# Prompt attention heads issued two at a time, and two key buffers exchanged, in a two-layer decoder step

## The chip, the core and the metric

The kernel runs on one core of a Trainium2 chip. The metric is the device time of one execution in microseconds (us), as a median over runs. The engines named are TensorE (PE for its matmuls, PEld for its weight loads), VectorE (DVE), ScalarE (ACT), GpSimd (POOL) and SyncE (SP, which here only issues transfers).

## What is computed

One inference step of a two-layer decoder for a prompt of 256 tokens and eight sequences of eight new tokens each, 320 tokens in all, with d_model 2048. A layer is an input projection, three mixers side by side, an output projection, and a feed-forward part:

```python
h   = rms_norm(x, norm1[l])
q, k, v, z, xbc, dt_raw, xp = jnp.split(h @ w_in[l], SPLITS, axis=-1)
o_sb   = stick_breaking_attention(q, k_all, v_all, pos0, sb_bias[l])   # 8 heads of 64
y_ssd  = ...   # Mamba2 chunked scan, 16 heads
y_pool = ...   # pooling over windows of 2, 4, 8, 16
x = x + jnp.concatenate([o_sb, y_ssd, y_pool], axis=-1) @ w_out[l]
x = x + (silu(conv3(rms_norm(x) @ w_gate)) * (rms_norm(x) @ w_up)) @ w_down
```

The attention has no softmax. For a query block, z = q k / 8 + bias, masked; the weight of a key is exp(log_sigmoid(z) + later), where `later` sums the masked log_sigmoid(-z) of the keys behind it; the output is weights times values. The prompt attends to itself; each of the eight sequences attends to 2048 cached keys and values as well, which lie in pages of 128 rows that a page table names.

## The kernel before

**Products.** Activations lie transposed, tiles of 128 features by 320 tokens. A weight block of 1024 by 256 numbers (1 MB) is a *unit*: SyncE loads it into one of four raw slots, ScalarE makes its rounded high part (`wh`), VectorE the rest (`wl`), and TensorE makes three products per 128x128 tile (L1183 to L1185: high by high, high by low, low by high), 48 instructions a unit. Four units are a *body*. `wh` and `wl` hold two units, so ScalarE and VectorE work a bounded way ahead of TensorE.

**Input stage of a layer.** Nine bodies follow one another: three of q, k, v, three of the scan's input, two of its gate, one of the pool's input (`B_XP`). Between the units, numbered u = 0 to 35 on every engine, the prompt's attention is done by a function `heads(u)` that each engine has for itself. For head n: TensorE makes the scores at u = 10 + 2n (`head_z`: a 256-column and a 128-column matmul over 64 partitions, into bank 4 or 5), VectorE copies them out with the bias at u = 12 + 2n (`head_in`, L1975, into one of four buffers `hbuf`), ScalarE takes the logarithms at 13 + 2n, VectorE the softplus at 14 + 2n, TensorE its running sums at 14 + 2n (`head_sums`, L1321 to L1324), VectorE the argument at 16 + 2n, ScalarE the exponential at 17 + 2n, TensorE the outputs at 18 + 2n (`head_out`, L1347 to L1349: three 128-column matmuls into one half of bank 7's partitions), and VectorE takes them at 20 + 2n (`head_take`). Every step waits by semaphore for the one before; the program order is fixed on each engine.

**Mixing stage.** Then the cached keys are gone through in 16 chunks of eight pages. A chunk's keys lie in one of two rings of eight pages: even chunks in `kring0`, over the later part of the residual x, odd ones in `kring1`, over raw slots 0 and 1. GpSimd stores the covered part of x to memory before (`x_stored`), SyncE brings it back after (`x_back`, L537). A page of keys is loaded into a ring slot once the page two chunks before has been transposed (`k_T`, counted over all pages; transposes at L1427). Values come page by page into one ring of eight, `vring`, from GpSimd's queue, each slot refilled once TensorE has used it (L1471). The scan's and the pool's steps are laid between by a table (`MIX`); among them L1529 and L1594.

**The way out.** The first body of w_out is loaded by SyncE in four transfers, `first_out(0)` to `first_out(3)`. The first two go to raw slots 0 and 1 and wait until chunk 15's first four, then all its pages have been transposed. The third waits for the last scores and arguments, then x comes back, then the engines meet and the fourth is issued. VectorE waits for `x_back` after that meeting, ahead of its split of the fourth (`out_lo(3)`, L2273).

Of the kernel before, what the change touches and what calls it, by code (L numbers as in the profile page):

```python
# [27 lines left out]
P = 128  # L28
# [102 lines left out]
def build(nc, a, o):  # L131

    with ExitStack() as ctx:
# [74 lines left out]
        kring = [sb_at("kring0", [P, RING, SBW], F32, x_at + 4096), sb_at("kring1", [P, RING, SBW], F32, raw_at)]  # L208
        x_late = x[:].rearrange("p k t -> p (k t)")[:, 1024:1024 + RING * SBW]
        x_kept = nc.dram_tensor("x_kept", (P, RING * SBW), F32, kind="Internal").ap()  # L210
# [219 lines left out]

        def tokens(blk):

            return (blk * P, P) if blk < 2 else (SEQ, SAMP)
# [6 lines left out]
        def _(sync):  # L440
# [21 lines left out]
            for l in range(DEPTH):  # L462
# [26 lines left out]
                for k in range(RING):  # L489
                    key_in(0, k)  # L490
# [13 lines left out]
                for q in range(1, CHUNKS):  # L504
                    for k in range(RING):
                        slot = RING * (q - 2) + k
                        if q == 1:
# [20 lines left out]
                sync.wait_ge(k_T, l * (CHUNKS * 8) + CHUNKS * 8 - 4)  # L528
                first_out(0)
                sync.wait_ge(k_T, l * (CHUNKS * 8) + CHUNKS * 8)  # L530
# [3 lines left out]
                first_out(2)  # L534
                for k in range(RING):
                    sync.wait_ge(v_loaded[k], (l + 1) * (16 * CHUNKS))
                sync.dma_start(x_late, x_kept).then_inc(x_back, 16)  # L537
# [29 lines left out]
        def _(pool):  # L567
# [37 lines left out]
            for l in range(DEPTH):  # L605
# [4 lines left out]
                pool.dma_start(x_kept, x_late).then_inc(x_stored, 16)  # L610
# [180 lines left out]
        def _(act):  # L791
# [104 lines left out]
            for l in range(DEPTH):  # L896
# [13 lines left out]
                def head_logs(n):  # L910
                    act.wait_ge(z_out, l * 8 + n + 1)
                    act.activation(za[:, n % 2, :], hbuf[:, n % 4, :], ACT.Abs)
# [3 lines left out]
                def head_weights(n):  # L916
                    act.wait_ge(z_arg, l * 8 + n + 1)
                    act.activation(hbuf[:, n % 4, :], hbuf[:, n % 4, :], ACT.Exp).then_inc(z_w, 1)
# [241 lines left out]
        def _(pe):  # L1160
# [87 lines left out]
            for l in range(DEPTH):  # L1248
# [55 lines left out]
                def head_z(n):  # L1304

                    pe.wait_ge(qk_ready, l + 1)
                    if n >= 2:
                        pe.wait_ge(z_out, l * 8 + (n - 1))
                    r, b = slice(DH * (n % 2), DH * (n % 2) + DH), ps[4 + n % 2]
                    pe.matmul(b[:, 0:SEQ], k[r, n // 2, 0:P], q[r, n // 2, 0:SEQ], start=True, stop=True)  # L1310
                    pe.matmul(b[:, SEQ:SEQ + P], k[r, n // 2, P:SEQ], q[r, n // 2, P:SEQ], start=True, stop=True
                              ).then_inc(z_mm, 1)
# [26 lines left out]
                def head_out(n):  # L1339
                    pe.wait_ge(z_w, l * 8 + (n + 1))  # L1340
                    if n:
                        pe.wait_ge(o_out, l * 8 + n)
# [1148 lines left out]
```

## Time and profile before

| | us |
|---|---|
| median of 3 runs | 3234.13 |
| lowest, highest | 3229.59, 3236.45 |
| profiled execution | 3232.32 |
| its span | 3230.7 |
| TensorE busy in the span | 3144.0 |
| VectorE, ScalarE busy | 1897.0, 1347.1 |

The profile gives, for one execution, each engine's busy time, the chain of waits that ended last (followed back from the last instruction to what released it), who waited for whom, and the instructions in order of time. In a timeline a line is start, duration, engine, line of the kernel, operation, output and inputs, shapes and count; in square brackets is the time that the engine stood idle before it and who ended that. Matmuls are pipelined: their durations overlap, and the distance of two starts is what one takes of the queue. One full matmul of 32-bit numbers leaves two records, a transpose one.

### The profile page before, as it was taken

To read this page: it belongs to the slowest core of one execution; us is meant where nothing else is said; L and a number is where in the kernel's file an instruction comes from. 1 tells how busy PE (TensorE), PEld (TensorE's weight loads), DVE (VectorE), ACT (ScalarE), POOL (GpSimd) and SP (SyncE) were. 2 spreads that over 40 slices of the span, in tenths; PEclk is the share of its full clock that TensorE was granted. 3 is DMA by queue.
4 is the path that set the end of the run, shared out by engine and by line. 5 is a ranking of instruction groups with operands and counts; after the bars stand their busy time and mean duration, and the time that the engine had idled before them with its cause. 6 is when DMAs were issued, how large, how long until landed. Compare 5 with 4: busy or idle time off the path is not lost.

```text
span 3230.7 us, 62291 instructions
## 1 busy us (share of the span) xinstructions
PE 3144.0 (97%) x23688; PEld 3005.7 (93%) x23688; DVE 1897.0 (59%) x3335; ACT 1347.1 (42%) x1663; POOL 432.7 (13%) x543
## 2 busy tenths in 40 slices
PE   8999998999999999999999999989999999999998
PEld 7999676999999999999999986769999999999998
DVE  5574756566654665466646647556666446644664
ACT  5463767334433333333335547653443333333332
POOL 0000755110000000000300026532000000000002
PEclk9999999999999999999999999999999999999999
DMA  7443899644444444444554448986444544454443
GB/s 225 137 136 121 259 324 335 210 155 143 153 148 149 150 151 150 154 150 135 159 167 131 157 128 273 339 295 192 146 151 145 158 144 156 143 156 146 146 146 107
DMA packets 470583, 562.73 MB, mean 174 GB/s; under 512 B 21343, under 2 KB 415296, under 8 KB 469764
## 3 DMA queue, kind: packets, MB, share of 16 engines
q1 hardware_dynamic: 442627, 471.26, 45.6%
q0 software_dynamic: 27392, 88.95, 7.9%
q8 instruction: 111, 1.82, 0.2%
q14 instruction: 68, 0.56, 0.0%
q10 hardware_dynamic: 385, 0.14, 0.0%
HBM read 539.69 MB, written 20.57 MB: 173 GB/s over the span
## 4 chain that ended last, share of the span: by engine, by line
PE 90%; DVE 3%; DMA 2%; ACT 1%; issue 1%; PEld 1%; DVEq 0%; ACTq 0%; PEldq 0%; SPq 0%; POOL 0%; POOLq 0%
PE ps L1183 26%; PE ps L1185 26%; PE ps L1184 26%; PE ps L1427 2%; PE ps L1471 1%; PE ps L1439 1%; DMA s_seq<-in_state_ssm 1%; PE ps L1581 1%; PE ps L1518 1%; PE ps L1594 0%; DMA raw<-in_w_out 0%; PE ps L1453 0%; PE ps L1575 0%; DVE kT L2091 0%; PE ps L1310 0%
## 5 line engine op out<-in xcount | busy, mean ns | idle before, releaser
L1710 DVE TENSOR_TENSOR wl<-raw,wh 128x1024 fp32r<-128x1024 f32 (+1 forms) x736 | 902.4, 1235 | 983.4 <-ACT wh L798 976.7
L798 ACT ACTIVATE wh<-raw 128x1024 fp32r<-128x1024 f32 (+1 forms) x736 | 764.8, 1041 | 1583.9 <-PE ps L1185 1572.3
L1183 PE MATMUL ps<-fh,wh 128*128 128x320 f32 x2816 | 870.6, 309 | 0.0
L1185 PE MATMUL ps<-fh,wl 128*128 128x320 f32 x2816 | 870.1, 309 | 0.0
L1184 PE MATMUL ps<-fl,wh 128*128 128x320 f32 x2816 | 870.1, 309 | 0.0
L1183 PEld LDWEIGHTS ps<-fh,wh 128*128 128x128 f32 x2816 | 528.5, 188 | 0.2
L1184 PEld LDWEIGHTS ps<-fl,wh 128*128 128x128 f32 x2816 | 528.5, 188 | 0.2
L1185 PEld LDWEIGHTS ps<-fh,wl 128*128 128x128 f32 x2816 | 528.5, 188 | 0.0
L1183 PE MATMUL ps<-ah,wh 128*128 128x320 f32 x1376 | 427.0, 310 | 0.0
L1185 PE MATMUL ps<-ah,wl 128*128 128x320 f32 x1376 | 425.2, 309 | 0.0
L1184 PE MATMUL ps<-al,wh 128*128 128x320 f32 x1328 | 410.3, 309 | 0.0
L1183 PE MATMUL ps<-hh,wh 128*128 128x320 f32 x1312 | 407.1, 310 | 0.4 <-DVE wl L1710 0.4
L1185 PE MATMUL ps<-hh,wl 128*128 128x320 f32 x1312 | 405.4, 309 | 0.0
L1184 PE MATMUL ps<-hl,wh 128*128 128x320 f32 x1264 | 390.5, 309 | 0.0
L1183 PEld LDWEIGHTS ps<-ah,wh 128*128 128x128 f32 x1376 | 258.3, 188 | 1.6 <-issue 0.3
L1185 PEld LDWEIGHTS ps<-ah,wl 128*128 128x128 f32 x1376 | 258.3, 188 | 0.0
L1184 PEld LDWEIGHTS ps<-al,wh 128*128 128x128 f32 x1328 | 249.3, 188 | 0.0
L1183 PEld LDWEIGHTS ps<-hh,wh 128*128 128x128 f32 x1312 | 246.2, 188 | 2.2 <-issue 1.0
L1185 PEld LDWEIGHTS ps<-hh,wl 128*128 128x128 f32 x1312 | 246.3, 188 | 0.0
L1184 PEld LDWEIGHTS ps<-hl,wh 128*128 128x128 f32 x1264 | 237.3, 188 | 0.0
L778 POOL DMA_DIRECT2D out_new_ffn_conv_prompt<-ftail x24 | 14.8, 616 | 1594.5 <-DVE ftail L1801 1594.5
L1427 PEld LDWEIGHTS ps<-con,kring 128*128 128x128 f32 x1024 | 116.6, 145 | 60.1 <-issue 58.6
(414 smaller groups left out, 3733.5 us busy)
## 6 DMA issues: line engine op xcount, KB each, us to landing
raw<-in_w_gate SPq DMA_DIRECT2D x88, 1024.0 KB, 5.0
raw<-in_w_up SPq DMA_DIRECT2D x88, 1024.0 KB, 5.0
raw<-in_w_in SPq DMA_DIRECT2D x72, 1024.0 KB, 5.2
kring<-in_cache_k SPq DMA_DIRECT2D x256, 256.0 KB, 4.5
vring<-in_cache_v POOLq DMA_DIRECT2D x256, 256.0 KB, 5.1
raw<-in_w_down SPq DMA_DIRECT2D x64, 1024.0 KB, 5.3
raw<-in_w_out SPq DMA_DIRECT2D x32, 1024.0 KB, 6.8
raw<-in_w_down SPq DMA_DIRECT2D x32, 768.0 KB, 4.6
```

What stands on the lines that cost most here:

```text
L778: pool.dma_start(new_p[i], ftail[part][32 * i:32 * i + 2, 0:tiles, :]).then_inc(tail_stored, 16)
L798: act.activation(wh[:, s % 2, half, :], raw[:, s, half, :], ACT.Copy).then_inc(hi_done, 1)
L1183: pe.matmul(out, wh[:, s % 2, kk, w], hi(row), start=first, stop=False)
L1184: pe.matmul(out, wh[:, s % 2, kk, w], lo(row), start=False, stop=False)
L1185: mm = pe.matmul(out, wl[:, s % 2, kk, w], hi(row), start=False, stop=last)
L1427: mm = pe.transpose(ps[4 + n % 2][:, j * P:(j + 1) * P], kring[q % 2][:, k, j * P:(j + 1) * P], ident)
L1439: mm = pe.matmul(ps[q % 2][32 * j:32 * j + 32, :], qp[:, q // 4, bb, j, :], kT[bb][:, j, :], start=(bb == 0), stop=(bb == 1))
L1471: mm = pe.matmul(ps[6][32 * j:32 * j + 32, 0:P], wz[:, k // 4, k % 4, j, :], vring[:, k, j * P:(j + 1) * P], start=False, stop=last)
L1518: mm = pe.matmul(bank[:, i * T:(i + 1) * T], tk[0:T, 1, h:h + 1].broadcast_to([T, P]), le, start=True, stop=True)
L1581: mm = pe.matmul(bank[:, j * 16:(j + 1) * 16].rearrange("p (e t) -> p e t", e=2), sT[:, i % 2, j * P:(j + 1) * P], csS[:, 2 * j:2 * j + 2, ...
L1710: dve.tensor_tensor(wl[:, s % 2, half, :], raw[:, s, half, :], wh[:, s % 2, half, :].bitcast(F32), ALU.subtract).then_inc(lo_done, 1)
```

## The change

TensorE's `head_z` and `head_out` become `pair_z` and `pair_out`. They handle two heads in one step, at every fourth u (10, 14, 18, 22 and 20, 24, 28, 32), with the matmuls of the two heads alternating. VectorE takes the outputs of two heads in one step, at 22, 26, 30, 34. Six score buffers are used in place of four; the two new ones, `hbuf_x`, lie over the first part of x, so the whole of x is now stored and brought back, and VectorE waits for that store before the first use of them (head 4).

The two key rings change places: even chunks lie over the raw slots, odd ones over x. So chunk 1 is loaded early and chunk 0 when the raw slots are free, and the first two transfers of w_out wait for chunk 14's transposes instead of chunk 15's. In the diff below the pure renamings of `hbuf[:, n % 4, :]` to `head_buf(l, n)` are left out.

```diff
@@ -205,9 +205,10 @@
-        kring = [sb_at("kring0", [P, RING, SBW], F32, x_at + 4096), sb_at("kring1", [P, RING, SBW], F32, raw_at)]
-        x_late = x[:].rearrange("p k t -> p (k t)")[:, 1024:1024 + RING * SBW]
-        x_kept = nc.dram_tensor("x_kept", (P, RING * SBW), F32, kind="Internal").ap()
+        kring = [sb_at("kring0", [P, RING, SBW], F32, raw_at), sb_at("kring1", [P, RING, SBW], F32, x_at + 4096)]
+        x_flat = x[:].rearrange("p k t -> p (k t)")
+        x_kept = nc.dram_tensor("x_kept", (P, KT * TOK), F32, kind="Internal").ap()
+        hbuf_x = sb_at("hbuf_x", [P, 2, 384], F32, x_at)
@@ -428,6 +429,10 @@
+        def head_buf(l, n):
...
+            return views[l].hbuf[:, n % 6, :] if n % 6 < 4 else hbuf_x[:, n % 6 - 4, :]
@@ -487,7 +492,7 @@
                 for k in range(RING):
-                    key_in(0, k)
+                    key_in(1, k)
                 body(l, B_XP, a["w_in"], 0, 8, XPC, XPC + 256)
@@ -501,10 +506,10 @@
-                for q in range(1, CHUNKS):
+                for q in (0, *range(2, CHUNKS)):
                     for k in range(RING):
                         slot = RING * (q - 2) + k
-                        if q == 1:
+                        if q == 0:
                             sync.wait_ge(lo_done, (l * BODIES + B_XP + 1) * 8 + 2 * (k // 4) + 2)
@@ -525,16 +530,17 @@
-                sync.wait_ge(k_T, l * (CHUNKS * 8) + CHUNKS * 8 - 4)
+                sync.wait_ge(k_T, l * (CHUNKS * 8) + CHUNKS * 8 - 12)
                 first_out(0)
-                sync.wait_ge(k_T, l * (CHUNKS * 8) + CHUNKS * 8)
+                sync.wait_ge(k_T, l * (CHUNKS * 8) + CHUNKS * 8 - 8)
                 first_out(1)
...
                 first_out(2)
+                sync.wait_ge(k_T, l * (CHUNKS * 8) + CHUNKS * 8)
                 for k in range(RING):
                     sync.wait_ge(v_loaded[k], (l + 1) * (16 * CHUNKS))
-                sync.dma_start(x_late, x_kept).then_inc(x_back, 16)
+                sync.dma_start(x_flat, x_kept).then_inc(x_back, 16)
                 for eng in ("pe", "dve", "pool"):
@@ -607,7 +613,7 @@
-                pool.dma_start(x_kept, x_late).then_inc(x_stored, 16)
+                pool.dma_start(x_kept, x_flat).then_inc(x_stored, 16)
@@ -1301,15 +1307,18 @@
-                def head_z(n):
+                def pair_z(m):
...
-                    if n >= 2:
-                        pe.wait_ge(z_out, l * 8 + (n - 1))
-                    r, b = slice(DH * (n % 2), DH * (n % 2) + DH), ps[4 + n % 2]
-                    pe.matmul(b[:, 0:SEQ], k[r, n // 2, 0:P], q[r, n // 2, 0:SEQ], start=True, stop=True)
-                    pe.matmul(b[:, SEQ:SEQ + P], k[r, n // 2, P:SEQ], q[r, n // 2, P:SEQ], start=True, stop=True
-                              ).then_inc(z_mm, 1)
+                    if m:
+                        pe.wait_ge(z_out, l * 8 + 2 * m)
+                    for e in range(2):
+                        r = slice(DH * e, DH * e + DH)
+                        pe.matmul(ps[4 + e][:, 0:SEQ], k[r, m, 0:P], q[r, m, 0:SEQ], start=True, stop=True)
+                    for e in range(2):
+                        r = slice(DH * e, DH * e + DH)
+                        pe.matmul(ps[4 + e][:, SEQ:SEQ + P], k[r, m, P:SEQ], q[r, m, P:SEQ], start=True, stop=True
+                                  ).then_inc(z_mm, 1)
@@ -1336,27 +1345,30 @@
-                def head_out(n):
-                    pe.wait_ge(z_w, l * 8 + (n + 1))
-                    if n:
-                        pe.wait_ge(o_out, l * 8 + n)
+                def pair_out(m):
+                    pe.wait_ge(z_w, l * 8 + (2 * m + 2))
+                    if m:
+                        pe.wait_ge(o_out, l * 8 + 2 * m)
                     else:
                         pe.wait_ge(v_tok_out, l * 3 + 2)
-                    r, b = slice(DH * (n % 2), DH * (n % 2) + DH), ps[7]
-                    w = hbuf[:, n % 4, :]
-                    pe.matmul(b[r, 0:P], v_tok[:, 0, n * DH:(n + 1) * DH], w[:, 0:P], start=True, stop=True)
-                    pe.matmul(b[r, P:SEQ], v_tok[:, 0, n * DH:(n + 1) * DH], w[:, P:SEQ], start=True, stop=False)
-                    pe.matmul(b[r, P:SEQ], v_tok[:, 1, n * DH:(n + 1) * DH], w[:, SEQ:384], start=False, stop=True
-                              ).then_inc(o_mm, 1)
+                    halves = [(ps[7][DH * e:DH * e + DH], slice((2 * m + e) * DH, (2 * m + e + 1) * DH), head_buf(l, 2 * m + e))
+                              for e in range(2)]
+                    for b, d, w in halves:
+                        pe.matmul(b[:, 0:P], v_tok[:, 0, d], w[:, 0:P], start=True, stop=True)
+                    for b, d, w in halves:
+                        pe.matmul(b[:, P:SEQ], v_tok[:, 0, d], w[:, P:SEQ], start=True, stop=False)
+                    for b, d, w in halves:
+                        pe.matmul(b[:, P:SEQ], v_tok[:, 1, d], w[:, SEQ:384], start=False, stop=True).then_inc(o_mm, 1)
...
-                    if u % 2 == 0 and 0 <= u - 18 < 16:
-                        head_out((u - 18) // 2)
+                    if u % 4 == 0 and 0 <= u - 20 < 16:
+                        pair_out((u - 20) // 4)
                     if u % 2 == 0 and 0 <= u - 14 < 16:
                         head_sums((u - 14) // 2)
-                    if u % 2 == 0 and 0 <= u - 10 < 16:
-                        head_z((u - 10) // 2)
+                    if u % 4 == 2 and 0 <= u - 10 < 16:
+                        pair_z((u - 10) // 4)
                     if u in (13, 15, 34):
@@ -1972,7 +1984,9 @@
                     dve.wait_ge(z_mm, l * 8 + n + 1)
-                    dve.scalar_tensor_tensor(hbuf[:, n % 4, :], ps[4 + n % 2][:, 0:384], hbias[:, n:n + 1],
+                    if n == 4:
+                        dve.wait_ge(x_stored, 16 * (l + 1))
+                    dve.scalar_tensor_tensor(head_buf(l, n), ps[4 + n % 2][:, 0:384], hbias[:, n:n + 1],
                                              con[:, K_NEG:K_NEG + 384], ALU.add, ALU.add).then_inc(z_out, 1)
...
@@ -2030,8 +2044,9 @@
                         value_rows((u - 15) // 2)
-                    if u % 2 == 0 and 0 <= u - 20 < 16:
-                        head_take((u - 20) // 2)
+                    if u % 4 == 2 and 0 <= u - 22 < 16:
+                        head_take((u - 22) // 2)
+                        head_take((u - 22) // 2 + 1)
                     if u % 2 == 0 and 0 <= u - 16 < 16:
```

## Rows read from the trace of the kernel before

**Rows 1.** Chain of waits of the whole span, its shares by engine.

```profile
PE 90%; DVE 3%; DMA 2%; ACT 1%; issue 1%; PEld 1%; DVEq 0%; ACTq 0%; PEldq 0%; SPq 0%; POOL 0%; POOLq 0%
```

**Rows 2.** TensorE's list of waits, two lines: waiter, cause, total us, times, longest.

```profile
PE ps L1471 <- DMA vring<-in_cache_v: 5.4, 7, 1.9
PE ps L1183 <- DVE wl L1710: 0.4, 1, 0.4
```

**Rows 3.** Timeline of TensorE, around a lone score step: start, us, instruction.

```profile
109.66 0.31 PE L1184 MATMUL ps<-hl,wh 128*128 128x320 f32 x1
109.81 0.31 PE L1185 MATMUL ps<-hh,wl 128*128 128x320 f32 x1
110.05 0.70 PE L1310 MATMUL ps<-qkv 64*128 64x256 f32 x2
110.59 0.38 PE L1311 MATMUL ps<-qkv 64*128 64x128 f32 x2
110.90 0.42 PE L1183 MATMUL ps<-hh,wh 128*128 128x320 f32 x1
111.15 0.31 PE L1184 MATMUL ps<-hl,wh 128*128 128x320 f32 x1
```

**Rows 4.** Timeline of TensorE, around a lone output step.

```profile
272.92 0.31 PE L1185 MATMUL ps<-hh,wl 128*128 128x320 f32 x1
273.16 0.43 PE L1347 MATMUL ps<-hbuf,v_tok 128*64 128x128 f32 x2
273.43 0.38 PE L1348 MATMUL ps<-hbuf,v_tok 128*64 128x128 f32 x2
273.65 0.38 PE L1349 MATMUL ps<-hbuf,v_tok 128*64 128x128 f32 x2
273.96 0.41 PE L1183 MATMUL ps<-hh,wh 128*128 128x320 f32 x1
```

**Rows 5.** Timeline of TensorE, first output matmul of heads 3, 4 and 5.

```profile
224.21 0.43 PE L1347 MATMUL ps<-hbuf,v_tok 128*64 128x128 f32 x2
241.22 0.43 PE L1347 MATMUL ps<-hbuf,v_tok 128*64 128x128 f32 x2
257.19 0.43 PE L1347 MATMUL ps<-hbuf,v_tok 128*64 128x128 f32 x2
```

**Rows 6.** Timeline of TensorE: column halves with what follows, then row halves likewise.

```profile
336.61 0.66 PE L1529 MATMUL ps<-seg,xtok 128*64 128x128 f32 x8
337.20 1.09 PE L1427 MATMUL ps<-con,kring 128*128 128x128 f32 x8
482.32 1.16 PE L1594 MATMUL ps<-bm,xw 64*128 64x128 f32 x16
483.41 0.64 PE L1471 MATMUL ps<-vring,wz 128*32 128x128 f32 x16
```

**Rows 7.** Timeline of VectorE, head 5's scores copied out.

```profile
196.18 0.61 DVE L1975 SCALAR_TENSOR_TENSOR hbuf<-ps,hbias,con 128x384 f32<-128x384 f32 x1
```

**Rows 8.** Timelines of SyncE, TensorE, VectorE: start and end of the mixing stage.

```profile
276.33 11.69 SPq L485 DMA_DIRECT2D kring<-in_cache_k  x8
313.99 1.04 PE L1427 MATMUL ps<-con,kring 128*128 128x128 f32 x8
531.16 1.09 PE L1427 MATMUL ps<-con,kring 128*128 128x128 f32 x8
545.91 6.26 SPq L445 DMA_DIRECT2D raw<-in_w_out  x2
588.31 2.36 DVE L2273 TENSOR_TENSOR wl<-raw,wh 128x1024 fp32r<-128x1024 f32 x2 [10.52 <-ACT wh L1067]
```

**Rows 9.** Busy time by stretch: us, engines, then granted clock, DMA share, GB/s.

```profile
560.00:565.00 5.00, 4.61 (x37) 3.51 (x38) 3.86 (x4) 3.92 (x4) 2.29 (x5) 0.66 0.89 274
```

**Rows 10.** The line that returns x: its issues, and its landing times.

```profile
L537 SPq DMA_DIRECT2D x<-x_kept x2: 338/340/343, 570.7 to 2167.3; - x2
DMA to landing us min/median/max: 7.8/8.3/8.9
```

More of the change, by code:

```diff
@@ L911, in head_logs @@
                     act.wait_ge(z_out, l * 8 + n + 1)
-                    act.activation(za[:, n % 2, :], hbuf[:, n % 4, :], ACT.Abs)
+                    act.activation(za[:, n % 2, :], head_buf(l, n), ACT.Abs)
                     act.drain()
@@ L917, in head_weights @@
                     act.wait_ge(z_arg, l * 8 + n + 1)
-                    act.activation(hbuf[:, n % 4, :], hbuf[:, n % 4, :], ACT.Exp).then_inc(z_w, 1)
+                    act.activation(head_buf(l, n), head_buf(l, n), ACT.Exp).then_inc(z_w, 1)
                 def heads(u):
@@ L1982, in head_softplus @@
                         dve.wait_ge(s_mm, l * 8 + n - 1)
-                    dve.scalar_tensor_tensor(sp[:, n % 2, :], hbuf[:, n % 4, :], 0.0, za[:, n % 2, :], ALU.max, ALU.add
+                    dve.scalar_tensor_tensor(sp[:, n % 2, :], head_buf(l, n), 0.0, za[:, n % 2, :], ALU.max, ALU.add
                                              ).then_inc(z_sp, 1)
@@ L1987, in head_argument @@
                     dve.wait_ge(s_mm, l * 8 + n + 1)
-                    dve.tensor_tensor(hbuf[:, n % 4, :], hbuf[:, n % 4, :], ps[6][:, 0:384], ALU.subtract
+                    dve.tensor_tensor(head_buf(l, n), head_buf(l, n), ps[6][:, 0:384], ALU.subtract
                                       ).then_inc(z_arg, 1)
```

## The prediction

> **What bounds the kernel now.** I read the chain of waits first: 90% of the span lies on TensorE [rows 1]. So TensorE's queue is the clock of this kernel, and whatever is taken out of that queue comes off the end, as long as nothing else becomes late. Next I read who TensorE waited for over the whole span. What is to be seen is what is absent: neither the score line of the prompt heads (L1310) nor their sums (L1321) nor their outputs (L1347) stands in that list, and the input products waited 0.4 us in all; the waits belong to the mixing stage, among them 5.4 us for value pages (vring) [rows 2]. Third, the timeline of TensorE around one head, to price it: product, product, the head's matmuls, products again [rows 3, 4]. The heads are islands in a stream of products, and each of them is on the path.
>
> **Part 1, heads in pairs: the price of one head now.** Products start 0.15 us apart (109.66, 109.81). Around a lone score step they start at 109.81 and 110.90, so 1.09 instead of 0.15, and the next one is 0.25 behind instead of 0.15: 0.94 + 0.10 = 1.04 us per head [rows 3]. Inside it the 256-column matmul holds the queue 0.54 and the 128-column one 0.31; about 0.2 is getting in and out. A lone output step: 272.92 to 273.96 is 1.04, less 0.15, plus the same 0.10 behind it, about 1.0 us per head, its three matmuls 0.22 to 0.31 apart [rows 4]. Beside other head work a step costs the same: 17.01 us lie between the outputs of heads 3 and 4, where a score step falls, and 15.97 between those of heads 4 and 5, where none does, again 1.04 for the score step [rows 5]. Eight heads, two layers: 16 x (1.04 + 1.0) = 32.6 us.
>
> **The same in pairs.** The diff issues the two heads' matmuls alternately: in the scores the operands lie on partitions 0 to 63 and 64 to 127 and the results go to banks 4 and 5, in the outputs the results go to the two halves of bank 7's partitions. The kernel already does both elsewhere. Row halves: L1594 alternates them, 8 matmuls of 64 rows x 128 columns (two records each) take 482.32 to 483.41 = 1.09 us. One by one they would take 0.05 + 8 x 0.22 = 1.81 (0.22 is 273.43 to 273.65 in the output step, 0.05 the dearer first one), four perfect pairs 0.05 + 4 x 0.22 = 0.93; so a pair costs 0.04 more than a single one [rows 4, 6]. Column halves: L1529 alternates them, 4 matmuls take 336.61 to 337.20 = 0.59, against 0.93 one by one and 0.49 in perfect pairs: 0.05 more per pair [rows 6]. So a second head in a score step costs 2 x 0.04 = 0.08, rounded to 0.1, and saves 1.04 - 0.1 = 0.94; in an output step it costs 3 x 0.05 = 0.15 and saves 1.0 - 0.15 = 0.85. Four pairs, two layers: 8 x 0.94 + 8 x 0.85 = 14.3 us. The bounds: all of the second head free, 16.3; nothing overlapped, so that the second head pays its plain streaming, 0.44 + 0.22 = 0.66 in the scores and 3 x 0.22 = 0.66 in the outputs, 8 x 0.38 + 8 x 0.34 = 5.8. I take 14.3, since L1594 and L1529 have these very tile shapes.
>
> A rule speaks against the output half. By the Trainium skill ("TensorE: Matmul & The Clock Gate", section "The mechanism" in Part 3) a weight load overlaps a running matmul only when its row group differs, and two column halves share their rows. By it the outputs would save 8 x 0.34 = 2.7 instead of 6.8 and part 1 would be 10.2 instead of 14.3. The row of L1529 disagrees (0.59 for four), and I go by the row.
>
> **New waits in part 1.** The scores of pair m wait until head 2m-1's scores are copied out of their bank, two head steps nearer than the same wait now; behind that wait stand the products. VectorE runs ahead of TensorE here: head 5's copy starts at 196.18 and takes 0.61, and the head step in which pair 3 will start begins one period of 17.01 before 224.21, at 207.2, so 10.4 us lie between them [rows 5, 7]. The outputs of a pair wait for weights that ScalarE makes one step earlier, as now. VectorE's two takes in a row are the same two copies as before; behind them wait its splits of the next weights, and the pair's outputs are issued two units earlier. Head 4's copy gains a wait for the store of x, which was issued before the first input products and which the key loads already wait for. I cost all of these at nothing; the cover is the 10.4 us, and each microsecond short of it would cost one at three pairs in each layer.
>
> **Part 2, the rings exchanged.** At the start chunk 1's keys now come early, and chunk 0's as soon as raw slots 0 and 1 have been split for the last input body. Now chunk 1's eight pages are issued at that point, 276.33 to 288.02, and TensorE first transposes keys at 313.99: 26 us of room, so nothing [rows 8]. At the end chunk 15 will lie over x, so the first two transfers of w_out wait for chunk 14's transposes (first half issued at 531.16) instead of chunk 15's, after which they are issued now, at 545.91 and about 552. They move some 13 us forward, out of the window in which TensorE waits for value pages (2.7 us a layer [rows 2]) and behind which the granted clock is 0.66 of full over 5 us, a mean of 1.2 and 2.4 GHz, after that idling [rows 8, 9]. At best all of it goes: 2.7 of waits and 5 x 0.34 = 1.7 of clock a layer. But the value pages come from GpSimd's queue into slots that TensorE itself frees; the moved transfers shorten their flight, not their start. I take 1.0 a layer, ends 0 and 4.4. On SP's queue the two pass nothing: the last keys are issued before them, and the third transfer keeps its waits for q_mm and q_arg. The store and the return of x grow from 4096 to 5120 words per partition, 2.1 to 2.6 MB. The return is issued at 570.7 and lands in about 8.3 us; a quarter more is 10.4, so 581.1 instead of 579 [rows 10]. VectorE waits for it ahead of out_lo(3), but stands there for ScalarE until 588.31, so 7 us of cover; what is left is its overlap with the fourth w_out transfer, 0 to 1 us a layer; I take 0.25 [rows 8, 10]. The store runs under the input products, which waited 0.4 us.
>
> **Sum.** 14.3 + 2 x 1.0 - 2 x 0.25 = 15.8. The profiled execution took 3232.3 (span 3230.7 and 1.6 around it), so 3216.5; the median of the three runs is 1.8 above it: **3218**.
>
> **Rivals.** (A) The change does not do what it says: halves do not overlap inside the stream of products; 5.8 from the pairs and 1.5 from the rings, 3227. Against it: L1594 and L1529 lie amid other work as well. (B) Only the column halves stay serial, the rule above: 15.8 - 4.1 = 11.7, 3222. For it: the outputs load six weights for six matmuls of 128 columns; against it L1529, which does the same. (C) Slower: the w_out transfers, then issued at about 532 and 540, meet the last keys and value pages, and the value pages of chunks 13 and 14 come late. The place is the last three chunks. The price: 1 MB each, at 2.1 MB in 8.3 us about 4 us of delay apiece. The ring holds one chunk, so a page is asked for about one chunk ahead of its use, some 13.5 us (from 532 to 545.9 TensorE goes from half of chunk 14 to half of chunk 15); it decides from the point at which a page flies longer than that. To end slower by 0.2% it must eat 15.8 + 6.5 = 22.3 us, 11 a layer, 3241; at 3 us a layer it gives 3224. For it speaks that TensorE waits for pages at all, against it that it waits 2.7 us a layer with the transfers in a worse place. (D) A head wait takes the place of the gain: VectorE's lead of 10.4 us gone at three pairs in two layers, 6 x 2.6 = 15.8, 3234. The trace speaks against it.
>
> **Chances and range.** Forecast 0.77, B 0.07, A 0.06, moderate C 0.03, full C 0.03, D 0.04. 0.2% of 3234 is 6.5 us, about what a measurement of this kernel can tell from no change: faster is below 3227.7. The forecast, B, moderate C and most of A lie there, less a little for wobble: faster 0.88, same 0.08, slower 0.04. Range: all second heads free (16.3) and 3 us a layer from the rings is 3212, so 3211; the high end is A with the rings worth nothing, 3228.
>
> **What would show it.** In the changed trace the heads' scores and outputs stand in four islands of two heads per layer; a score pair takes about 1.15 us out of the products instead of 2.1, an output pair about 1.15 instead of 2.0, and TensorE's list of waits is still without them. The stretch from the first scores to the end of the input products is shorter by about 7 us in each layer. In the mixing stage the first w_out transfers are issued about 13 us earlier, and the waits for vring fall below 5.4 us. The prediction is wrong if a pair takes as long as two heads (A, B), if a wait on z_out or o_out appears on TensorE (D), or if waits for vring grow before chunk 15 (C).

## The result and the profile after

Median 3215.3 us (3212.41 to 3220.31, 6 runs) against 3232.31 us for the kernel before, timed beside it on the same chip (6 runs): a ratio of 0.9945, 95% interval 0.9926 to 0.9963, faster by 17.0 us. The profiled execution took 3212.93 us with a span of 3211.3; 3216.5 had been forecast for it, and 3218 for the median.

The chain of waits by engine, and three lines of what TensorE waited for (total us, times, longest us), kernel after:

```profile
PE 89%; DVE 2%; DMA 2%; ACT 1%; issue 1%; POOL 1%; PEld 1%; DVEq 1%; ACTq 0%; POOLq 0%; PEldq 0%; SPq 0%
...
PE ps L1483 <- DMA vring<-in_cache_v: 6.0, 6, 2.5
PE ps L1631 <- DVE wl L2288: 4.2, 2, 2.3
...
PE ps L1189 <- DVE wl L1722: 0.4, 1, 0.4
```

TensorE is still the chain [rows 1]. In the list neither the paired scores (L1317, L1320), nor their sums (L1330 to L1333), nor the paired outputs (L1358 to L1362) appear, and the input products still wait 0.4 us [rows 2]: the added head waits cost nothing that shows. The value pages wait 6.0 us where they waited 5.4.

TensorE's timeline after, around the first score pair and around an output pair (start us, us of the group from first start to last end, what, count of records; two records for each matmul of the heads):

```profile
109.88 0.31 PE L1191 MATMUL ps<-hh,wl 128*128 128x320 f32 x1
110.12 0.70 PE L1317 MATMUL ps<-qkv 64*128 64x256 f32 x4
110.65 0.39 PE L1320 MATMUL ps<-qkv 64*128 64x128 f32 x4
110.97 0.42 PE L1189 MATMUL ps<-hh,wh 128*128 128x320 f32 x1
111.22 0.31 PE L1190 MATMUL ps<-hl,wh 128*128 128x320 f32 x1
...
279.96 0.31 PE L1191 MATMUL ps<-hh,wl 128*128 128x320 f32 x1
280.20 0.44 PE L1358 MATMUL ps<-hbuf,v_tok 128*64 128x128 f32 x4
280.47 0.39 PE L1360 MATMUL ps<-hbuf,v_tok 128*64 128x128 f32 x4
280.69 0.39 PE L1362 MATMUL ps<-hbuf,v_tok 128*64 128x128 f32 x4
281.00 0.41 PE L1189 MATMUL ps<-hh,wh 128*128 128x320 f32 x1
```

From product to product a score pair takes 110.97 - 109.88 = 1.09 us and an output pair 281.00 - 279.96 = 1.04 us. These are, to the hundredth, what one head took before [rows 3, 4]. The second head is free on row halves (the scores) and on column halves (the outputs).

### Where the difference lies, stretch by stretch

I cut both traces at three places of each layer: the first score matmul, the first transpose of the new keys (L1401 before, L1413 after), and the history transposes (L1667, L1679). The input stretch runs from the first to the second, the mixing stage from the second to the third. Their ends in layer 0, in TensorE's timelines before and after (the starts are at 110.05 and 110.12, above):

```profile
312.65 0.73 PE L1401 MATMUL ps<-con,qkv 128*128 128x128 f32 x5 [1.79 <-DVEq L379]
610.91 2.24 PE L1667 MATMUL ps<-con,frow 16*128 16x16 f32 x44
```

```profile
304.63 0.85 PE L1413 MATMUL ps<-con,qkv 128*128 128x128 f32 x6 [1.79 <-DVEq L380]
602.81 2.23 PE L1679 MATMUL ps<-con,frow 16*128 16x16 f32 x44
```

So the input stretch went from 312.65 - 110.05 = 202.6 to 304.63 - 110.12 = 194.5 us, 8.1 less, and so it did in layer 1. Four heads fewer to pay at 1.04 + 1.0 [rows 3 to 5] are 8.2. The mixing stage took 298.3 and then 298.2 us in layer 0, 303.4 and then 298.7 in layer 1; and 1.5 us were lost behind the history transposes of layer 0 (below). 2 x 8.1 + 0.1 + 4.7 - 1.5 = 19.5, against 19.4 between the spans. The two questions for the experiments follow: is the input gain really the halves of the array, and does the 4.7 us in layer 1's mixing stage come from the exchanged rings?

### The profile page after: what moved, and what is told of

Same layout as the page of the kernel before. It is cut to its first block, busy times and chain, and to the rows that moved or that the text cites. A ratio compares the mean times of both kernels' runs of the same rounds, so it can differ in the third digit from the quotient of the medians.

```text
span 3211.3 us, 62279 instructions
## 1 busy us (share of the span) xinstructions
PE 3123.2 (97%) x23688; PEld 2990.9 (93%) x23688; DVE 1897.4 (59%) x3335; ACT 1346.8 (42%) x1663; POOL 431.2 (13%) x543
## 4 chain that ended last, share of the span: by engine, by line
PE 89%; DVE 2%; DMA 2%; ACT 1%; issue 1%; POOL 1%; PEld 1%; DVEq 1%; ACTq 0%; POOLq 0%; PEldq 0%; SPq 0%
PE ps L1189 26%; PE ps L1190 26%; PE ps L1191 26%; PE ps L1439 2%; PE ps L1483 1%; PE ps L1451 1%; DMA s_seq<-in_state_ssm 1%; PE ps L1593 1%; PE ps L1530 0%; DMA raw<-in_w_out 0%; DMA vring<-in_cache_v 0%; PE ps L1465 0%; PE ps L1606 0%; PE ps L1587 0%; DVEq L2119 0%
## 5 line engine op out<-in xcount | busy, mean ns | idle before, releaser
L1439 PEld LDWEIGHTS ps<-con,kring 128*128 128x128 f32 x1024 | 116.0, 145 | 61.0 <-issue 59.5
```

What stands on the lines that cost most here:

```text
L1439: mm = pe.transpose(ps[4 + n % 2][:, j * P:(j + 1) * P], kring[q % 2][:, k, j * P:(j + 1) * P], ident)
```

## Experiments

Each kernel left a trace, cut in the same way. "Clock loss" is the sum, over windows of 10 us of the mixing stage, of one minus the granted clock, times the length; "rest" is the stage less that loss. For the kernel before in layer 0 it comes from these windows, in each of which the clock was not full all the time (window, length, busy us of each engine with its count, granted clock, DMA share, GB/s):

```profile
320.00:330.00 10.00, 9.09 (x64) 7.65 (x63) 7.52 (x19) 6.81 (x10) 3.58 (x7) 0.83 0.95 305
...
440.00:450.00 10.00, 5.28 (x66) 3.66 (x64) 6.77 (x6) 7.15 (x10) 5.49 (x7) 0.91 1.07 363
450.00:460.00 10.00, 10.00 (x76) 8.09 (x74) 1.13 (x3) 2.45 (x5) 1.07 (x2) 0.58 1.02 344
...
560.00:570.00 10.00, 9.61 (x72) 8.51 (x73) 3.86 (x4) 4.58 (x6) 3.36 (x7) 0.83 0.95 321
```

That is 1.7 + 0.9 + 4.2 + 1.7 = 8.5 us. The 0.58 is 2.4 GHz for a sixth of the window and 1.2 GHz for the rest, after a window in which TensorE was busy for 5.28 of 10 us.

| kernel (trace) | input stretch, per layer | mixing, layer 0 (clock loss, rest) | mixing, layer 1 (clock loss, rest) | 1.5 us lost behind history transposes, layers 0, 1 | span |
|---|---|---|---|---|---|
| before | 202.6 | 298.3 (8.5, 289.8) | 303.4 (15.3, 288.1) | no, no | 3230.7 |
| before, second trace | 202.6 | 294.9 (5.1, 289.8) | 303.4 (15.3, 288.1) | no, no | 3227.3 |
| before, third trace | 202.6 | 299.0 (11.9, 287.1) | 301.4 (13.7, 287.7) | no, no | 3230.8 |
| pairs alone | 194.5 | 299.5 (10.3, 289.2) | 307.5 (15.4, 292.1) | yes, yes | 3224.2 |
| rings alone | 202.6 | 304.5 (18.9, 285.6) | 298.0 (10.2, 287.8) | no, no | 3231.5 |
| after | 194.5 | 298.2 (8.5, 289.7) | 298.7 (8.5, 290.2) | yes, no | 3211.3 |
| after, second trace | 194.5 | 296.7 (6.8, 289.9) | 301.7 (11.9, 289.8) | no, no | 3210.8 |
| after, third trace | 194.5 | 298.9 (11.9, 287.0) | 294.1 (5.2, 288.9) | no, yes | 3207.4 |
| not alternated | 195.6 | 297.0 (6.8, 290.2) | 302.9 (17.1, 285.8) | yes, yes | 3217.5 |
| one half | 197.1 | 302.5 (15.3, 287.2) | 295.9 (5.1, 290.8) | no, yes | 3217.6 |
| fourth transfer early | 194.5 | 306.4 (18.7, 287.7) | 293.7 (6.8, 286.9) | no, yes | 3214.5 |
| the same, second trace | 194.5 | 304.8 (17.1, 287.7) | 297.0 (12.0, 285.0) | yes, no | 3216.7 |

### The two parts of the change, each alone

Pairs alone: the changed kernel with the rings, the key order and the waits for keys as before.

```diff
-        kring = [sb_at("kring0", ..., raw_at), sb_at("kring1", ..., x_at + 4096)]
+        kring = [sb_at("kring0", ..., x_at + 4096), sb_at("kring1", ..., raw_at)]
-                    key_in(1, k)
+                    key_in(0, k)
-                for q in (0, *range(2, CHUNKS)):
+                for q in range(1, CHUNKS):
-                sync.wait_ge(k_T, l * (CHUNKS * 8) + CHUNKS * 8 - 12)
+                sync.wait_ge(k_T, l * (CHUNKS * 8) + CHUNKS * 8 - 4)
-                sync.wait_ge(k_T, l * (CHUNKS * 8) + CHUNKS * 8 - 8)
+                sync.wait_ge(k_T, l * (CHUNKS * 8) + CHUNKS * 8)
```

> The heads in pairs, the rings as before (the whole of x is still stored and returned). Theory (pairs carry the gain): the stretch from the first scores to the first key transposes of a layer is 194.5 us as in the changed kernel, against 202.6 before, so 16.2 us for two layers, and the time lies 14 to 17 us below the kernel before, ratio 0.995. Rival 1 (the rings carry a good part, since the mixing stage of layer 1 took 4.7 us less in the changed kernel's trace): the stretch is 194.5 as well, but the time is only 10 to 12 us below, and layer 1's mixing stage (first key transposes to the history transposes of the feed-forward part) is back at 303. Rival 2 (part of the pairs' gain is given back at the stage's end): mixing stages longer than 298 and 303 by some us.

Measured: 3222.59 us (12 runs) against 3231.49 (29 runs), ratio 0.9974, 0.9960 to 0.9988. The input stretch came out as expected, 194.5, so 16.2 us less in two layers. The time did not: 8.9 us less (3.9 to 12.9), below the theory's 14 to 17 and also below rival 1's 10 to 12. Nearest comes rival 2: the mixing stages were longer than 298 and 303, by 1.5 and 4.5 us. What is known of it stands at the end of the account below.

Rings alone: the kernel before with those lines exchanged, the heads one by one and the store of x as it was.

> The rings exchanged and the two w_out transfers earlier, the heads one by one as before. Theory (as predicted): 1.0 us a layer, less 0.25 (nothing here, x returns in its old size): 1 to 2 us below the kernel before, ratio 0.9995, which is within what can be told; the input stretch 202.6 as before. Rival 1 (the earlier transfers leave the value pages as late as before, since their start is set by the ring and the GpSimd queue): the waits for vring stay at 5.4 to 6 us in both layers together, time within 1 us of before. Rival 2 (the rings bring the 4.7 us that layer 1's mixing stage lost): 4 to 6 us below, and that stage at 298 to 299 again.

Measured: 3232.15 us (12 runs) against the same 3231.49: ratio 1.0000, 0.9988 to 1.0011. Input stretch 202.6. SyncE's issue of the first two w_out transfers moved as the diff says, and TensorE's wait for pages is what it was (kernel with the rings alone; SyncE's timeline, TensorE's waits):

```profile
538.08 6.85 SPq L445 DMA_DIRECT2D raw<-in_w_out  x2
...
PE ps L1472 <- DMA vring<-in_cache_v: 5.0, 5, 2.9
```

The issue lies 7.8 us earlier than the 545.91 of before, in a stage that lost 18.9 us to the clock instead of 8.5. The exchange by itself brings nothing that can be measured: between 3.9 us won and 3.6 lost. That doesn't tell the theory's 1 to 2 us from rival 1's nothing; rival 2's 4 to 6 us are excluded.

The changed kernel again, beside those two:

> The changed kernel once more, on the same chip as the others. If the 4.7 us of layer 1's mixing stage belong to the change, that stage takes 298 to 299 us here too, and the stretches in which the granted clock is under full speed lie at the same places. If they belong to where the clock happens to fall in one execution, the stage takes another time, by up to 5 us, at equal waits, and the places of low clock differ. The time: ratio to before 0.9945 as at first, 0.993 to 0.996; the difference to the kernel with pairs alone is under 3 us.

Measured: 3219.34 us (3207.34 to 3232.07, 12 runs), ratio 0.9964, 0.9949 to 0.9978. In this trace layer 1's mixing stage took 301.7, not 298.7, with 11.9 of clock loss instead of 8.5, in part at other places. The 4.7 us of the first comparison are clock. That the rings caused it is not shown: layer 1 lost 13.7 to 15.4 us in the four traces with the rings as before and 5.1 to 17.1 in the eight with them exchanged, layer 0 the other way round (5.1 to 11.9 and 6.8 to 18.9), and the rings alone won no time. With the rings the pairs gave 3219.3, without them 3222.6, 3.25 us where under 3 was expected, and the ratio just misses the expected 0.993 to 0.996; the intervals overlap, so what the rings are worth to the paired kernel is left open between nothing and a few us.

### The kernel before, traced twice more

No edit; the question was whether the mixing stage of the kernel before varies as well, and whether it too falls behind the history transposes.

> The kernel before once more, for its trace alone: how its mixing stages (298.3 and 303.4 us in the first trace) and its clock vary from one execution to the next. Theory (the clock falls at places that change from one execution to the next, in either kernel alike): input stretches 202.6 again, mixing stages again 288 to 290 plus what the granted clock falls short, the sum of that 5 to 19 us per stage as in the changed kernel; the fall behind the 44 history transposes (1.5 us, seen in about half of the layers of the kernels with pairs) appears here too in some layer. Rival (the kernels with pairs lose more clock, which is where a part of their 16.2 us went): at most 10 us per stage here, and no fall behind the history transposes.

> The same, a third trace of the kernel before. Theory and rival as in the run beside it: input stretches 202.6; the mixing stages 288 to 290 plus 5 to 19 us of clock and now and then a fall behind the history transposes (theory), or never more than 10 us and never that fall (rival).

Measured: 3229.0 and 3232.49 us. The stage varies: 294.9 to 303.4 over six stages, with 5.1 to 15.3 of clock loss. The rest was 287.1 and 287.7 in the third trace, just below the theory's 288 to 290. But the six never lost time behind the history transposes, so the rival had half of it: that loss was seen with the pairs alone.

### What makes the second head free

Not alternated: all matmuls of one head of a pair, then all of the other.

```diff
                     for e in range(2):
                         r = slice(DH * e, DH * e + DH)
                         pe.matmul(ps[4 + e][:, 0:SEQ], ...)
-                    for e in range(2):
-                        r = slice(DH * e, DH * e + DH)
                         pe.matmul(ps[4 + e][:, SEQ:SEQ + P], ...).then_inc(z_mm, 1)
...
                     for b, d, w in halves:
                         pe.matmul(b[:, 0:P], ...)
-                    for b, d, w in halves:
                         pe.matmul(b[:, P:SEQ], ...)
-                    for b, d, w in halves:
                         pe.matmul(b[:, P:SEQ], ...).then_inc(o_mm, 1)
```

> The changed kernel with the same pairs, halves and waits, but the matmuls of a pair in another order: first all of the one head, then all of the other. Theory (two halves run side by side only where the matmuls that use them are neighbours in TensorE's queue): in the scores the second head's 256 columns can begin beside the first head's 128, so a pair holds the queue about 0.43 us longer than alternated (0.85 becomes about 1.3); in the outputs only the first head's third and the second head's first matmul overlap, 0.8 becomes about 1.24. The stretch from the first scores to the first key transposes grows from 194.5 to about 198.0 a layer. Rival 1 (the queue looks further ahead and overlaps them anyway): 194.5. Rival 2 (no overlap at all without alternation): 194.5 + 4 x 0.66 + 4 x 0.66 = 199.8.

Measured: 3219.13 us, input stretch 195.6 in both layers, 1.1 per layer more: neither the theory's 3.5, nor rival 1's nothing, nor rival 2's 5.3. TensorE's timeline of that kernel, a score pair, an output pair, and two loads of weights from the place of the latter:

```profile
140.09 0.71 PE L1317 MATMUL ps<-qkv 64*128 64x256 f32 x4
140.62 0.39 PE L1318 MATMUL ps<-qkv 64*128 64x128 f32 x4
140.95 0.41 PE L1189 MATMUL ps<-hh,wh 128*128 128x320 f32 x1
...
280.23 0.31 PE L1191 MATMUL ps<-hh,wl 128*128 128x320 f32 x1
280.47 0.43 PE L1356 MATMUL ps<-hbuf,v_tok 128*64 128x128 f32 x2
280.74 0.27 PE L1357 MATMUL ps<-hbuf,v_tok 128*64 128x128 f32 x1
280.74 0.32 PE L1356 MATMUL ps<-hbuf,v_tok 128*64 128x128 f32 x1
...
280.96 0.27 PE L1358 MATMUL ps<-hbuf,v_tok 128*64 128x128 f32 x1
...
281.23 0.38 PE L1358 MATMUL ps<-hbuf,v_tok 128*64 128x128 f32 x2
281.54 0.42 PE L1189 MATMUL ps<-hh,wh 128*128 128x320 f32 x1
...
280.63 0.25 PEld L1357 LDWEIGHTS ps<-hbuf,v_tok 128*64 128x64 f32 x2
280.74 0.19 PEld L1356 LDWEIGHTS ps<-hbuf,v_tok 128*64 128x64 f32 x2
```

L1356 is the first matmul of a head, L1357 the second, L1358 the third. At 280.74 an L1356 starts beside the L1357 of the first head, and at 280.96 follows the first head's L1358: the second head began ahead of a matmul that stands before it in the program. So TensorE looked ahead here and filled the other column half by itself; only about one matmul at each end stays alone, and the pair takes 281.54 - 280.23 = 1.31 instead of 1.04. The 0.27, four times a layer, is 1.1, the whole difference of the stretch. The scores, on row halves, took 0.86 us from their first matmul to the next product in this order (140.09 to 140.95) and 0.85 in the changed kernel: there the order makes no difference. All four records of L1317, of both heads, come ahead of L1318, although the program has the first head's L1318 between them. Both my theory (only neighbours overlap) and rival 1 (the order doesn't matter) are wrong for the outputs; for the scores rival 1 is right.

One half: the outputs of both heads into the same half of bank 7's partitions, in two column ranges, one head after the other.

```diff
-                    halves = [(ps[7][DH * e:DH * e + DH], ...) for e in range(2)]
+                    halves = [(ps[7][0:DH, SEQ * e:SEQ * e + SEQ], ...) for e in range(2)]
-                    dve.wait_ge(o_mm, l * 8 + n + 1)
-                    dve.tensor_copy(q[r, n // 2, 0:SEQ], ps[7][r, 0:SEQ])
+                    dve.wait_ge(o_mm, l * 8 + (n | 1) + 1)
+                    dve.tensor_copy(q[r, n // 2, 0:SEQ], ps[7][0:DH, SEQ * (n % 2):SEQ * (n % 2) + SEQ])
```

with the loops of the previous kernel in the outputs.

> The changed kernel, scores alternated as there, but both heads' outputs go to the same half of bank 7's partitions, side by side in its columns, one head after the other; the copies then wait for both. Theory (the halves are what makes the second head free): an output pair holds the queue 3 x 0.22 = 0.66 us longer, and the input stretch grows from 194.5 to 197.1 a layer. Rival (the pair's gain is that there are fewer islands in the stream of products, the halves add little): 195 or less.

Measured: 3219.21 us, input stretch 197.1 in both layers, 2.6 more per layer, as expected. TensorE's timeline of that kernel:

```profile
281.47 0.31 PE L1191 MATMUL ps<-hh,wl 128*128 128x320 f32 x1
281.71 0.43 PE L1358 MATMUL ps<-hbuf,v_tok 128*64 128x128 f32 x2
...
282.41 0.38 PE L1358 MATMUL ps<-hbuf,v_tok 128*64 128x128 f32 x2
...
283.16 0.42 PE L1189 MATMUL ps<-hh,wh 128*128 128x320 f32 x1
```

Here the second head begins at 282.41 and pays 0.22 for each of its matmuls: 283.16 - 281.47 = 1.69 us for two heads. Four pairs x (1.69 - 1.04) = 2.6. The kernel not alternated issues in the same order, on two halves, and takes 1.31, so for the outputs it is the two halves that make the second head free. No run put both heads' scores on one row half; for them it is read from the records, where two heads take the time of one. Sharing one island alone saves little: two islands cost 2 x 0.99 and this one 1.69 - 0.15 + 0.10 = 1.64, so 0.34 per pair, the prediction's lower bound for the outputs.

### A version that goes on: the fourth w_out transfer early

The trace after shows TensorE waiting 4.2 us in two places for VectorE's splits of the output weights (L1631 above), which wait for the fourth w_out transfer, issued only behind the meeting of the engines. This kernel issues it right behind the return of x, with the waits that its target needs:

```diff
                 sync.dma_start(x_flat, x_kept).then_inc(x_back, 16)
+                body_steps(sync, l, B_OUT, 2)
+                sync.wait_ge(s_bm, l * NB + NB)
+                sync.wait_ge(s_decayed, l * NB + NB)
+                first_out(3)
                 for eng in ("pe", "dve", "pool"):
                     sync.wait_ge(at_stage[eng], stage(l, M_MIX))
-                first_out(3)
```

> The changed kernel, and the fourth w_out transfer is issued right behind the return of x, as soon as the products that read raw slot 3's place are done, and not after the engines have met. Theory (the transfer's 6.6 us and the splits behind it end 1.9 and 2.3 us after TensorE's other products in the two layers): that wait on VectorE's split is gone, and the low clock that followed it in layer 0 with it; 4 to 6 us below the changed kernel. Rival (the transfer then shares the queues with the return of x, 2.6 MB, which VectorE waits for ahead of its split): the wait stays or only changes its name, within 1 us of the changed kernel.

Measured: 3209.09 us (6 runs), ratio to before 0.9933, 0.9919 to 0.9947; the changed kernel beside it 3219.34. Again, in another comparison:

> The changed kernel with the fourth w_out transfer issued behind the return of x, once more, beside the changed kernel itself on one chip. Theory: TensorE's wait on the split of that transfer (1.9 and 2.3 us in the two layers of the changed kernel) is gone, so it lies 4 to 6 us below the changed kernel in this call, ratio to the kernel before 0.993 to 0.995. Rival (the 10 us between the two in the first call were the places where the granted clock fell): within 2 us of the changed kernel.

> The changed kernel, timed beside the one above. Theory: the input stretches are 194.5 us in each layer in every execution, and what varies is the mixing stage, which takes 288 to 290 us plus 10 us times the sum of what the granted clock falls short of full in its 10 us stretches; in this execution as well. The time 10 to 16 us below the kernel before. Rival: the mixing stage varies by its waits (transfers), and the sum does not hold within 2 us.

Measured: 3212.62 us (6 runs), ratio 0.9922, 0.9899 to 0.9945; the changed kernel 3218.33 (8 runs), ratio 0.9952, 0.9933 to 0.9972. So 10.2 and 5.7 us faster than the changed kernel, where 4 to 6 was expected; the intervals part in the first comparison and overlap in the second. The traces bear the expected size out: from the first w_out product to the history transposes (552.69 to 602.81 in the first trace after) it is 49.95 us a layer in the mean of the changed kernel's three traces and 47.3 in the two traces here, so 5.3 us in two layers. What the first comparison shows beyond that is open. The run of the changed kernel had 194.5 in both layers as expected, and rests of 287.0 and 288.9, one of them below the 288 to 290 of the theory; the rival's 2 us were not reached. The wait itself, in TensorE's timeline of the changed kernel (third trace):

```profile
582.27 0.41 PE L1631 MATMUL ps<-hh,wh 128*128 128x320 f32 x1 [2.47 <-DVE wl L2288]
```

and what took its place with the transfer early, in TensorE's waits and VectorE's timeline:

```profile
PE ps L1634 <- issue: 0.7, 2, 0.4
...
585.64 2.36 DVE L2291 TENSOR_TENSOR wl<-raw,wh 128x1024 fp32r<-128x1024 f32 x2 [6.83 <-ACT wh L1076]
```

TensorE no longer waits for the split (L1634 is the L1631 of this kernel). By the medians it is the fastest of the kernels here.

## Why the prediction was right, point by point

**The islands, and the halves: right in kind, too small in size.** The forecast charged a second head 0.1 us in a score pair and 0.15 in an output pair and had 14.3 us for both layers. Measured: 0 in both, and 16.2, the upper bound of that part. The mis-sized term is the 0.04 or 0.05 per pair from [rows 6]. There 0.16 and 0.10 us above perfect pairs were divided by the number of pairs in the island; but the excess is the island's edge, and a lone step has it too. By the same formula the lone output step of [rows 4] would take 0.05 + 3 x 0.22 = 0.71 us from its first matmul to the next product; it takes 273.96 - 273.16 = 0.80, so 0.09 more with no second head in it. That is the 0.10 of L1529, and most of the 0.16 of L1594.

The rule weighed in the prediction (the Trainium skill, "TensorE: Matmul & The Clock Gate", section "The mechanism" in Part 3) lets a weight load overlap a running matmul only when its row group differs. As the prediction read it, the output pair would be serial but for its island's edges, some 1.7 us, as the kernel with one half has it; the pair takes 1.04. The traces do not agree with the rule itself either: in the kernel not alternated the weights of L1356 are loaded at 280.74 while a matmul on the same rows starts. But so are the weights of L1357 at 280.63, on the same rows and columns as the L1356 that is running then, so loads under running matmuls are not what the halves add. What they add is that two matmuls run side by side. In this kernel column halves overlap as well as row halves do.

**The new waits: right.** None of the head lines is in TensorE's list after.

**The rings: right on the transfers, wrong on the waits; their worth in time is not settled.** SyncE issued the first two w_out transfers at 524.15 after; the 545.91 of before [rows 8], less the 8.0 that the input stretch lies earlier by then, is 537.9, so 13.8 us earlier, as forecast (13). The flight of the value pages shortened too: DMA issues of the last 17 us of mixing, before and then after (count, KB each, median us to landing):

```profile
vring<-in_cache_v POOLq DMA_DIRECT2D x14, 256.0 KB, 5.3
```

```profile
vring<-in_cache_v POOLq DMA_DIRECT2D x13, 256.0 KB, 3.2
```

The step that failed is the forecast that the waits for vring would fall: 5.4, 5.9 and 6.2 us in the three traces before, 6.0, 5.7 and 5.8 in the three after, 5.0 with the rings alone. The prediction had named the reason, that the moved transfers do not change when a page is asked for, but its sum did not use it. Of rival (C) nothing shows: the long waits still lie at the end, in chunk 15. After, GpSimd's timeline and TensorE's, at the end of mixing:

```profile
547.37 0.54 POOL L635 DMA_DIRECT2D vring<-in_cache_v  x1 [1.15 <-PE ps L1483]
548.53 0.54 POOL L635 DMA_DIRECT2D vring<-in_cache_v  x1 [0.62 <-PE ps L1483]
...
547.56 1.66 PE L1483 MATMUL ps<-vring,wz 128*32 128x128 f32 x48 [0.35 <-ACT wz L995]
551.67 0.43 PE L1483 MATMUL ps<-vring,wz 128*32 128x128 f32 x8 [2.45 <-DMA vring<-in_cache_v]
552.33 0.43 PE L1483 MATMUL ps<-vring,wz 128*32 128x128 f32 x8 [0.24 <-DMA vring<-in_cache_v]
552.69 0.41 PE L1631 MATMUL ps<-y_hi,o_h 128*128 128x320 f32 x1
```

The last two pages can only be asked for when TensorE's own L1483 frees their slots, 1.16 us apart. From the last weight transposes to the first w_out product it was 562.05 - 553.87 = 8.18 us before and 552.69 - 545.12 = 7.57 after. This holds over all traces: 8.0 to 9.5 us, mean 8.8, in the eight layers with the rings as before, and 7.2 to 8.6, mean 8.0, in the 16 with the rings exchanged. So 0.8 us a layer is won at this place, near the 1.0 of the sum, though not by shorter waits. In the layers named the granted clock over it was 0.93 before and 1.00 after, so the clock is a likely reason; no run shows it alone. Behind it a part is lost again: from the first w_out product to the history transposes it is 49.4 us with the rings as before and 49.9 with them exchanged (the kernels of the early fourth transfer left out).

**The return of x: right in its time, its cost not settled.** A quarter more bytes took 8.8 and 9.7 us in the first trace after and up to 10.4 in the other two, not 8.3; 10.4 had been allowed. TensorE's wait behind it (L1619 before, L1631 after) was 3.4 to 3.8 us in three traces before and 4.1 to 4.8 in three after, so in the mean 0.8 us more in two layers, 0.4 a layer; 0.25 was taken. The kernel with the rings alone, whose return carries the old 4096 words, waited 4.9; the kernels not alternated and with one half, with the larger return and the rings exchanged, waited 3.4 and 3.7. So neither the bytes nor the order of the transfers is shown to be the reason.

**What the sum did not have.** The mixing stage of any of these kernels lasts 294 to 308 us, and most of that difference is clock: 5 to 19 us of loss, 285 to 292 of rest (mean 288.4 over six stages before, 289.3 over six after). One comparison of spans is therefore good to about 10 us, and so the timed gains of the changed kernel were 17.0, 12.2 and 17.1 us around a fixed 16.2. Second, the loss behind the history transposes, in 9 of 16 layers of kernels with pairs and in 0 of 8 without; TensorE's timeline after and, for comparison, before:

```profile
602.81 2.23 PE L1679 MATMUL ps<-con,frow 16*128 16x16 f32 x44
604.98 0.49 PE L1189 MATMUL ps<-y_hi,wh 128*128 128x320 f32 x1
605.26 0.47 PE L1190 MATMUL ps<-y_lo,wh 128*128 128x320 f32 x1
605.53 0.47 PE L1191 MATMUL ps<-y_hi,wl 128*128 128x320 f32 x1
```

```profile
613.07 0.42 PE L1183 MATMUL ps<-y_hi,wh 128*128 128x320 f32 x1
613.33 0.31 PE L1184 MATMUL ps<-y_lo,wh 128*128 128x320 f32 x1
613.47 0.31 PE L1185 MATMUL ps<-y_hi,wl 128*128 128x320 f32 x1
```

After, products start 0.27 us apart instead of 0.15, half the pace, until about 608.5; the clock of the window from 600 to 610 is 0.83, so a third of it was granted at 1.2 GHz (with 2.4 for the rest). It costs 1.5 us where it happens (1092.1 instead of 1090.6 us from there to the next layer's scores), about 1.7 us an execution of a kernel with pairs. Why only kernels with pairs show it is open.

**How it came out right.** The pairs were 1.9 us too small, and 1.7 us were lost behind the history transposes, which the sum did not have. That these two cancel is luck. For the rings and the return of x the sum had 1.5 us; by the stretches above they are worth 0.8 - 0.5 = 0.3 a layer, and the timing cannot tell either from nothing. 15.8 was forecast, 16.2 less 1.7 is about 14.5 by the pairs' stretches, and 12 to 17 was timed. The forecast's 3218 lies between the changed kernel's three medians, 3215.3, 3219.3 and 3218.3. The least explained of the runs is the one with pairs alone: of its 16.2 us the timing shows 8.9. Its trace has 3.0 lost behind the history transposes and a rest of 292.1 in layer 1, the longest here. Its two waits for s_seq, 5.4 us together, don't explain it: the kernel before had 5.3. From the last weight transposes to the history transposes its two layers take 59.5 us each, against 57.7 in the mean of the three traces before, so 3.6 us more; with the 3.0 that would leave 9.6 of the 16.2, near what was timed. It is one trace, and why it is slower there is open.

## What to carry to other kernels

Price a small step in a stream of products from product to product, with its edges, and then ask what a second one costs inside the same island: on two halves of the array, by rows or by columns, it cost nothing here. Before a freed stretch of DMA time is counted as gain, look at what sets the start of the transfer that is waited for, not only at its flight. And before a few us between two executions are explained, put the granted clock of each stage beside them, over several executions of both kernels.

## What the hardware showed that I had not expected

- TensorE started matmuls out of program order when they used the other half of the array: on column halves a second head's first matmul at 280.74, the first head's third at 280.96; on row halves both heads' L1317 ahead of either L1318.
- Behind the 44 history transposes (16 rows each), during which TensorE's records show it busy for 2.23 us without a gap, products ran at half pace, at a granted clock of 0.83 over the 10 us window, in 9 of 16 layers of the kernels with pairs and in none of 8 of those without.
- The granted clock cost 5 to 19 us in a mixing stage of about 300, at places that in part change from one execution of the same kernel to the next.
